# A transformer kernel of twenty stages on one core: norm and setup at the program's start reordered, and three weight splits of the sliding attention moved

## The chip, the cores and the metric

One core of a Trainium2 chip runs the whole program. The metric is the device time of one execution in microseconds (us); the kernel before has a median of 2272.48 us over three runs (2271.74 to 2279.61).

## What is computed

Four blocks one after the other over x of 512 tokens by 1024 features, float32: a sparse attention (nsa) and a differential attention, then an RWKV mixer with a feed-forward layer and a sliding-window attention with a second feed-forward layer. Cut to what the change touches: the first norm (with norm_pre[0]) and the sliding attention, in which `band` gives each block of 128 keys together with the one before:

```python
def rmsnorm(x, g):
    xf = x.astype(jnp.float32)
    y = xf * lax.rsqrt(jnp.mean(xf * xf, axis=-1, keepdims=True) + EPS)
    return (y * g.astype(jnp.float32)).astype(x.dtype)

def swa_sink_attention(x, k, v, w_q, sinks, w_o):
    q = (x @ w_q).reshape(B, nb, BLOCK, KV_HEADS, GROUP, HEAD_DIM)
    kb, vb = band(k), band(v)
    s = jnp.einsum('bnqhgd,bnkhd->bnhgqk', q, kb).astype(jnp.float32) * (HEAD_DIM ** -0.5)
    s = jnp.where(mask[None, :, None, None], s, NEG_INF)
    m = jnp.maximum(jnp.max(s, axis=-1, keepdims=True), sk)
    p = jnp.exp(s - m)
    denom = jnp.sum(p, axis=-1, keepdims=True) + jnp.exp(sk - m)
    o = jnp.einsum('bnhgqk,bnkhd->bnqhgd', (p / denom).astype(vb.dtype), vb)
    return o.reshape(B, T, ATTN_HEADS * HEAD_DIM) @ w_o
```

Beside that, a table of 32 relative-distance biases is spread over distances with a one-hot matrix for the first two attentions.

## The kernel before

**Split products.** Every float32 operand of a projection is held as two fp32r parts: a high part (rounded by ScalarE) and a low part (the rest, by GpSimd for weights and by VectorE for activations). A projection multiplies high with high, low with high and high with low (`project_features`, L334 to L361: 24 matmuls of 128x512 for each weight load of 128 columns; `project_tokens` for outputs by token). Weights come in loads of 512 KB into a ring of three raw slots (`fetch`, L255, on the SP queue, which waits for the low split of the load that had the slot). ScalarE's `split_hi` (L266, the instruction at L278) and GpSimd's `split_lo` (L282, at L289) fill a ring of three pairs of parts. A part's slot is reused when the projection three loads back is done. Where the calls to `split_hi` and `split_lo` stand in each engine's program decides when each load is split.

**Stages.** The program is a list of stages, each with a method for TensorE (`tensor`), ScalarE (`scalar`), VectorE (`vector`) and GpSimd (`gpsimd`). Behind each stage every engine signals; unless a flag such as `scalar_goes_on` is set, it then waits for the other three (`end_stage`, L3186).

**The start.** `Setup` (L503) loads x (2 MB, one load), constants, the bias table and the one-hot matrix, and sixteen small pieces of vectors into rows (L528 to L549), splits the table in three bf16 parts on VectorE, and turns the rows with six transposes (L559) and copies (L595). Then, behind a barrier, `Norm` (L694) runs: GpSimd issues the load of the gain (L629); for each of the four tiles of 128 tokens ScalarE squares (L634), takes the root (L636) and scales (L654), VectorE multiplies with the gain (L644) and inverts (L649), TensorE turns the tile with eight transposes (L663), ScalarE makes the high part (L673) and VectorE the low part (L681). Behind another barrier the first projection begins (`NsaProject`, L931). After its first twelve weight loads TensorE makes the biases: eight groups of 32 small matmuls (L571) in banks 4 to 7, each copied out by VectorE (L602).

**The sliding attention.** `SwaProject` (L2046) makes the queries: eight weight loads, with the first two pairs' scores ahead of the last one. `SwaAttend` (L2098) then goes over 32 pairs u (eight pairs of heads by four blocks of 128 queries, the block without a predecessor last). For each: two score matmuls per pair of heads (L2134, TensorE), masked minimum on VectorE (L2256), exponential on ScalarE (L2143), reciprocal of the sum on VectorE (L1310), scaling on GpSimd (L2234; `sink` at L2227 puts the sink column in), transposes on TensorE (`turn`, L2156, three pairs behind the scores), a copy by VectorE (L2265) or ScalarE (L2199), values on TensorE (L2168, one more pair behind). Every fourth pair the result is split in high (L2203) and low (L2269). At the steps 11, 19 and 27 ScalarE and GpSimd each split one of the first three loads of the output's weights:

```python
    SPLITS = [11, 19, 27]
...
            if u in self.SPLITS:
                self.env.split_lo(pool, self.ahead - 2 + self.SPLITS.index(u))
            if u < n_pairs:
                sink(u)
            if u >= 2:
                scale(u - 2)
```

The next stage, `Output` (L727), multiplies with those weights, slice by slice (L386 high parts, L396 low part), beginning when the last low part of the attention's result is there.

Of the kernel before, what the change touches and what calls it, by code (L numbers as in the profile page):

```python
# [14 lines left out]
P = 128  # L15
T = 512
# [486 lines left out]
class Setup(Stage):  # L503


    def __init__(self, env):
        super().__init__(env)
        self.bias = env.take(HEADS, T, at=env.words - HEADS * T)
        at = env.area
        self.rows = env.take(6, P, at=at)  # L510
        self.tab = env.take(HEADS, at=at + 1000)
        self.tab_rest = env.take(HEADS, at=at + 1016)
# [3 lines left out]
        self.x_arrived = env.sem("x_arrived")  # L516
# [35 lines left out]
    def tensor(self, pe):  # L552
        env, nc = self.env, self.env.nc
        pe.wait_ge(self.rows_arrived, 16 * self.N_ROWS)
        pe.wait_ge(self.const_arrived, 16)
        pe.wait_ge(self.tab_arrived, 64)
        for n in range(6):
            size = [128, 56, 88, 88, 88, 88][n]
            tr = nc.tensor.transpose(env.ps[:, n // 4, (n % 4) * P:(n % 4) * P + size], self.rows[0:size, n, :],  # L559
                                     env.ident[0:size, 0:size])  # L560
# [14 lines left out]
    def vector(self, dve, step):  # L575
        env, nc = self.env, self.env.nc
        nc.vector.memset(env.eps, EPS)
        nc.vector.memset(self.tab[:], 0.0).then_inc(self.rows_zeroed, 1)
        dve.wait_ge(self.tab_arrived, 64)
        dve.wait_ge(self.rows_zeroed, 1)  # L580

# [8 lines left out]
        nc.vector.memset(self.table3[96:128, :], NEG).then_inc(self.table_ready, 1)  # L590
        dve.wait_ge(self.vec_ready, 1)
        o = 0
        for n in range(6):
            size = [128, 56, 88, 88, 88, 88][n]
            step(nc.vector.tensor_copy(env.vec[:, o:o + size], env.ps[:, n // 4, (n % 4) * P:(n % 4) * P + size]))  # L595
            o += size

# [13 lines left out]
class Renorm:  # L611
# [27 lines left out]
    def gain(self, dve, i):  # L639

        env, nc = self.env, self.env.nc
        if self.g_row is not None:
            dve.wait_ge(env.next_g_arrived, 16 * self.g_n)
            nc.vector.tensor_tensor(self.un[:, i, :], env.x[:, i, :], env.next_g, ALU.mult)  # L644

# [48 lines left out]
class Norm(Stage):  # L694


    def __init__(self, env, g_row, u, x_arrived):
        super().__init__(env)
        self.norm, self.x_arrived = Renorm(env, g_row, u), x_arrived
# [5 lines left out]
    def scalar(self, act, step):  # L705
        act.wait_ge(self.x_arrived, 16)
        for i in range(NT):
            self.norm.square(act, step, i)
            self.norm.unit(act, i)
        self.env.split_hi(act, 1)  # L710
        for i in range(NT):
            self.norm.high(act, i)

    def vector(self, dve, step):
        for i in range(NT):
            self.norm.gain(dve, i)
            self.norm.invert(dve, i)
        for i in range(NT):
            self.norm.low(dve, i)

    def tensor(self, pe):
        for i in range(NT):
# [208 lines left out]
class NsaProject(Stage):  # L931
# [19 lines left out]
    def tensor(self, pe):  # L951
        env, nc = self.env, self.env.nc
        u = self.m.u
        for ld, g in self.q + self.kvc:
            project_features(env, pe, ld, u, g)
        self.setup.bias_tensor(pe)

        pe.wait_ge(self.setup.bias_taken, 8)
# [7 lines left out]
    def vector(self, dve, step):  # L966
        self.setup.bias_vector(dve, step)
# [900 lines left out]
class FfnUp(Stage):  # L1868
# [4 lines left out]
    def __init__(self, env, layer, m):  # L1873
# [9 lines left out]
        n = str(layer)  # L1883
        self.scaled, self.scaled_before = m.scaled, 2 * FT * layer
        self.gelu_done, self.gelus_before = m.gelu_done, FT * layer
        self.product_ready = env.sem("product_ready" + n)
        self.act_hi_ready, self.act_done = env.sem("act_hi_ready" + n), env.sem("act_done" + n)
# [5 lines left out]
    def wait_result(self, pe, k):  # L1893
        pe.wait_ge(self.act_done, k + 1)
# [13 lines left out]
    def scalar(self, act, step):  # L1908
        env, nc, m = self.env, self.env.nc, self.m

        def gelu(j):
            act.wait_ge(env.proj_taken, self.g0 + 2 * j + 2)
            if j >= 2:
                act.wait_ge(self.act_done, j - 1)
            nc.scalar.activation(m.gelu[:, j % 2, :], m.conv[:, 2 * (j % 2), :], ACT.Gelu_apprx_tanh).then_inc(self.gelu_done, 1)

        def act_hi(j):
            act.wait_ge(self.product_ready, j + 1)
# [1400 lines left out]
```

## Time and profile before

| | |
|---|---|
| median of three runs | 2272.48 us |
| profiled execution: its time / its span | 2274.92 us / 2273.0 us |
| TensorE busy | 2070.1 us, 91% |
| ScalarE / VectorE / GpSimd busy | 41% / 37% / 40% |
| mean granted TensorE clock | 0.937 of 2.4 GHz |
| share of the last chain on TensorE | 79% |

TensorE's busy time is the length of the program but for a tenth. An engine's idle time matters only where TensorE waits for it. In the rows, PE is TensorE, ACT ScalarE, DVE VectorE, POOL GpSimd, SP the queue of the loads.

### The profile page before, as it was taken

To read this page: it belongs to the slowest core of one execution; us is meant where nothing else is said; L and a number is where in the kernel's file an instruction comes from. 1 tells how busy PE (TensorE), PEld (TensorE's weight loads), DVE (VectorE), ACT (ScalarE), POOL (GpSimd) and SP (SyncE) were. 2 spreads that over 40 slices of the span, in tenths; PEclk is the share of its full clock that TensorE was granted. 3 is DMA by queue.
4 is the path that set the end of the run, shared out by engine and by line. 5 is a ranking of instruction groups with operands and counts; after the bars stand their busy time and mean duration, and the time that the engine had idled before them with its cause. 6 is when DMAs were issued, how large, how long until landed. Compare 5 with 4: busy or idle time off the path is not lost.

```text
span 2273.0 us, 33586 instructions
## 1 busy us (share of the span) xinstructions
PE 2070.1 (91%) x13582; PEld 1661.5 (73%) x13582; DVE 848.5 (37%) x1813; ACT 935.9 (41%) x1707; POOL 915.2 (40%) x636
## 2 busy tenths in 40 slices
PE   4999999999997968997588899999999899999998
PEld 3889756788765746776477588888878568888886
DVE  2100467340027375146565353333033524334301
ACT  3431477453247354443133353444143535344422
POOL 2431267534446322341012734455434542544542
PEclk9987999999998969898589999999999999999999
DMA  4322100123310211221210323333322121333332
GB/s 119 93 78 65 47 20 2 48 69 101 93 56 19 70 42 49 76 75 38 49 31 19 101 62 98 102 93 111 102 75 84 38 66 56 102 97 98 103 111 74
DMA packets 222361, 161.05 MB, mean 71 GB/s; under 512 B 30631, under 2 KB 205295, under 8 KB 222208
## 3 DMA queue, kind: packets, MB, share of 16 engines
q1 hardware_dynamic: 220016, 151.83, 22.6%
q0 software_dynamic: 2192, 7.07, 1.0%
q8 instruction: 109, 1.79, 0.3%
q14 instruction: 44, 0.36, 0.1%
HBM read 153.64 MB, written 5.24 MB: 70 GB/s over the span
## 4 chain that ended last, share of the span: by engine, by line
PE 79%; DVE 9%; ACT 4%; POOL 3%; issue 3%; DMA 1%; POOLq 1%; SPq 0%; DVEq 0%; PEld 0%; PEldq 0%; ACTq 0%
PE ps L386 15%; PE ps L348 13%; PE ps L350 13%; PE ps L359 13%; PE ps L396 7%; PE ps L1355 2%; PE ps L1368 2%; PE ps L1344 2%; POOL weights_lo L289 1%; DVE ps L901 1%; DVE buffer L906 1%; PE ps L1082 1%; PE ps L2892 1%; PE ps L2156 1%; PE ps L1703 1%
## 5 line engine op out<-in xcount | busy, mean ns | idle before, releaser
L289 POOL TENSOR_TENSOR weights_lo<-buffer,weights_hi 128x1024 fp32r<-128x1024 f32 (+1 forms) x265 | 654.0, 2470 | 981.4 <-ACT weights_hi L278 981.2
L278 ACT ACTIVATE weights_hi<-buffer 128x1024 fp32r<-128x1024 f32 (+1 forms) x265 | 276.4, 1045 | 340.7 <-PE ps L396 285.5
L348 PE MATMUL ps<-u_hi,weights_hi 128*128 128x512 f32 (+1 forms) x752 | 278.5, 378 | 5.6 <-DVE u_lo L681 3.0
L350 PE MATMUL ps<-u_lo,weights_hi 128*128 128x512 f32 (+1 forms) x736 | 274.8, 377 | 0.0
L1931 ACT ACTIVATE buffer<-ps,buffer 128x512 f32<-128x512 f32 x88 | 68.7, 781 | 276.4 <-PE ps L359 276.4
L359 PE MATMUL ps<-u_hi,weights_lo 128*128 128x512 f32 (+1 forms) x752 | 177.2, 378 | 0.0
L1961 DVE SCALAR_TENSOR_TENSOR buffer<-ps,buffer,buffer 128x511 f32<-128x511 f32 x88 | 66.0, 750 | 287.7 <-ACT buffer L1931 287.7
L348 PEld LDWEIGHTS ps<-u_hi,weights_hi 128*128 128x128 f32 x752 | 141.2, 190 | 32.0 <-issue 5.6
L350 PEld LDWEIGHTS ps<-u_lo,weights_hi 128*128 128x128 f32 x736 | 138.4, 188 | 25.5
L359 PEld LDWEIGHTS ps<-u_hi,weights_lo 128*128 128x128 f32 x752 | 137.0, 191 | 25.8
L2932 ACT ACTIVATE buffer<-ps 32x256 f32<-32x256 f32 (+5 forms) x96 | 47.7, 498 | 152.9 <-PE ps L2892 68.1
L386 PE MATMUL ps<-weights_hi,act_hi 128*128 128x512 f32 x352 | 108.8, 390 | 0.5 <-issue 0.5
L386 PE MATMUL ps<-weights_hi,act_lo 128*128 128x512 f32 x352 | 108.4, 389 | 0.0
L1430 POOL TENSOR_SCALAR buffer<-buffer,buffer,buffer 128x512 f32<-128x512 f32 (+3 forms) x128 | 76.4, 609 | 41.2 <-DVE buffer L1310 41.2
L396 PE MATMUL ps<-weights_lo,act_hi 128*128 128x512 f32 x352 | 92.8, 389 | 0.0
L900 DVE RECIPROCAL buffer<-buffer 128x1 f32<-128x1 f32 x24 | 3.9, 162 | 230.8 <-ACT buffer L827 230.7
L348 PE MATMUL ps<-nsa_u_hi,weights_hi 128*128 128x512 f32 x192 | 82.7, 431 | 7.5 <-PEq L3188 5.7
L1389 ACT ACTIVATE buffer<-buffer,buffer 128x512 f32<-128x512 f32 (+3 forms) x128 | 71.4, 558 | 30.1 <-DVE buffer L1463 29.2
L350 PE MATMUL ps<-nsa_u_lo,weights_hi 128*128 128x512 f32 x192 | 80.6, 420 | 0.0
L348 PE MATMUL ps<-diff_u_hi,weights_hi 128*128 128x512 f32 (+1 forms) x216 | 77.6, 373 | 3.3 <-ACT weights_hi L278 2.2
L386 PEld LDWEIGHTS ps<-weights_hi,act_hi 128*128 128x128 f32 x352 | 65.7, 188 | 15.5 <-issue 2.1
L1463 DVE CUSTOM_DVE_ANT_0 buffer<-ps,buffer 128x512 f32<-128x512 f32 (+3 forms) x128 | 61.9, 486 | 38.3 <-PE ps L1344 36.0
(403 smaller groups left out, 4277.5 us busy)
## 6 DMA issues: line engine op xcount, KB each, us to landing
buffer<-in_w_up SPq DMA_DIRECT2D x88, 512.0 KB, 3.8
buffer<-in_w_down SPq DMA_DIRECT2D x44, 512.0 KB, 3.4
buffer<-in_diff_w_in SPq DMA_DIRECT2D x32, 512.0 KB, 4.0
buffer<-in_nsa_w_in SPq DMA_DIRECT2D x28, 512.0 KB, 3.8
buffer<-in_w_rkv SPq DMA_DIRECT2D x24, 512.0 KB, 4.1
buffer<-in_nsa_w_out SPq DMA_DIRECT2D x8, 512.0 KB, 3.5
buffer<-in_diff_w_out SPq DMA_DIRECT2D x8, 512.0 KB, 3.6
buffer<-in_w_o_rwkv SPq DMA_DIRECT2D x8, 512.0 KB, 3.4
```

Source lines behind the costliest of these rows:

```text
L278: self.nc.scalar.activation(self.part_hi[:, part % self.PARTS, 0:n], self.raw[:, ld % self.RAW, 0:n], ACT.Copy).then_inc(self.hi_ready, 1)
L289: self.nc.gpsimd.tensor_tensor(self.part_lo[:, part % self.PARTS, 0:n], self.raw[:, ld % self.RAW, 0:n], self.part_hi[:, part % self.PARTS ...
L348: nc.tensor.matmul(out, hi[:, k, :], rhs[0][:, k, tokens], start=(k == 0), stop=False)
L350: nc.tensor.matmul(out, hi[:, k, :], rhs[1][:, k, tokens], start=False, stop=False)
L359: mm = nc.tensor.matmul(out, lo[:, k, :], rhs[0][:, k, tokens], start=False, stop=(k == KD - 1))
L386: nc.tensor.matmul(out(i, b), lhs[part][:, index * m + k, i * P:(i + 1) * P], hi[:, k, b * width:(b + 1) * width], start=(index + k == 0 a ...
L396: mm = nc.tensor.matmul(out(i, b), lhs[0][:, index * m + k, i * P:(i + 1) * P], lo[:, k, b * width:(b + 1) * width], start=False, stop=stop)
L1389: nc.scalar.activation(m.p[:, at, 0:n], m.p[:, at, 0:n], ACT.Exp, scale=-1.0, bias=m.nmax[:, at:at + 1], accum_out=m.psum[:, at:at + 1]).t ...
L1430: nc.gpsimd.tensor_scalar(p, p, m.scale[:, at:at + 1], m.gate[:, i, gate:gate + 1], ALU.mult, ALU.mult).then_inc(self.p_scaled, 1)
L1463: nc.vector.tensor_tensor_reduce(m.p[:, at, 0:n], self.banks(u)[:, st, 0:n], m.bias[:, 2 * k + st, T - n:T], -1.0, 1e38, ALU.add, ALU.min, ...
L1931: nc.scalar.activation(m.conv[:, 2 * (j % 2) + half, :], env.bank(g), ACT.Identity, scale=self.col(2, half, j), bias=self.col(3, half, j)) ...
L1961: step(nc.vector.scalar_tensor_tensor(c[:, 1:T], env.bank(g)[:, 0:T - 1], self.col(1, half, j), c[:, 1:T], ALU.mult, ALU.add))
```

## The change

At the start: x comes in three loads, the first three weights are fetched ahead of the small loads (`load_vectors`), the first two stages have no barrier, and ScalarE loads the root's table at once. VectorE scales a tile with gain and reciprocal in one instruction (`scale`), in place of ScalarE's `unit` and VectorE's `gain`. The table's preparation, the rows' transposes (now in banks 6 and 7) and their copies move into `NsaProject`, ahead of the biases. The scratch of `Setup` moves to another place in memory.

In the sliding attention: the split at step 11 moves into the query projection behind the last query weight's split (j = 6), those at 19 and 27 behind the last pair. In `FfnUp` both layers share five semaphores, which count on (`tiles_before`); no instruction moves there.

```diff
@@ Setup
-        self.x_arrived = env.sem("x_arrived")
+        self.tensor_goes_on = self.scalar_goes_on = self.vector_goes_on = self.gpsimd_goes_on = True
+        self.x_arrived = [env.sem(f"x_arrived{i}") for i in range(3)]
...
     def load(self, sp):
         env, io, nc = self.env, self.env.io, self.env.nc
-        sp.dma_start(env.x, io["x"].rearrange("b (t p) d -> p (b t) d", p=P)).then_inc(self.x_arrived, 16)
-        sp.dma_start(env.const, io["shape_constants"]).then_inc(self.const_arrived, 16)
+        for i, end in enumerate((1, 2, NT)):
+            sp.dma_start(env.x[:, i:end, :],
+                         io["x"][0, i * P:end * P, :].rearrange("(t p) d -> p t d", p=P)).then_inc(self.x_arrived[i], 16)
+            if i == 0:
+                sp.dma_start(env.const, io["shape_constants"]).then_inc(self.const_arrived, 16)
+
+    def load_vectors(self, sp):
+        io = self.env.io
         sp.wait_ge(self.rows_zeroed, 1)
...
     def bias_tensor(self, pe):
 
         env, nc = self.env, self.env.nc
+        pe.wait_ge(self.tab_arrived, 64)
+        pe.wait_ge(self.table_ready, 1)
         for i in range(8):
-            if i >= 4:
-                pe.wait_ge(self.bias_taken, i - 3)
+            if i >= 2:
+                pe.wait_ge(self.bias_taken, max(i - 2, 1))
...
+    def scale(self, dve, i):
+
+        env, nc = self.env, self.env.nc
+        dve.wait_ge(env.next_g_arrived, 16 * self.g_n)
+        dve.wait_ge(env.rstd_ready, self.n + i + 1)
+        nc.vector.scalar_tensor_tensor(self.un[:, i, :], env.x[:, i, :], self.rstd[:, i:i + 1], env.next_g,
+                                       ALU.mult, ALU.mult).then_inc(env.un_ready, 1)
@@ Norm
+        self.tensor_goes_on = self.scalar_goes_on = self.vector_goes_on = self.gpsimd_goes_on = True
...
     def scalar(self, act, step):
-        act.wait_ge(self.x_arrived, 16)
-        for i in range(NT):
-            self.norm.square(act, step, i)
-            self.norm.unit(act, i)
-        self.env.split_hi(act, 1)
-        for i in range(NT):
-            self.norm.high(act, i)
+        env, norm = self.env, self.norm
+        act.wait_ge(self.setup.rows_zeroed, 1)
+        env.nc.scalar.activation(env.sqrt_junk, env.eps, ACT.Sqrt)
+
+        def square(i):
+            act.wait_ge(self.setup.x_arrived[min(i, 2)], 16)
+            norm.square(act, step, i)
+
+        for i in range(3):
+            square(i)
+        norm.high(act, 0)
+        square(3)
+        norm.high(act, 1)
+        env.split_hi(act, 0)
+        norm.high(act, 2)
+        norm.high(act, 3)
+        env.split_hi(act, 1)
 
     def vector(self, dve, step):
         for i in range(NT):
-            self.norm.gain(dve, i)
             self.norm.invert(dve, i)
-        for i in range(NT):
-            self.norm.low(dve, i)
+            self.norm.scale(dve, i)
+            if i:
+                self.norm.low(dve, i - 1)
+        self.norm.low(dve, NT - 1)
@@ NsaProject
         for ld, g in self.q + self.kvc:
             project_features(env, pe, ld, u, g)
+        self.setup.vectors_tensor(pe)
         self.setup.bias_tensor(pe)
...
     def vector(self, dve, step):
+        self.setup.table_vector(dve, step)
+        self.setup.vectors_vector(dve, step)
         self.setup.bias_vector(dve, step)
@@ SwaProject
-        self.env.split_lo(pool, self.q[-1][0])
+        self.env.split_lo(pool, self.q[-1][0] + 1)
...
-            env.split_hi(act, min(ld + 1, self.q[-1][0]))
+            env.split_hi(act, min(ld + 1, self.q[-1][0]) + (j >= KD - 2))
@@ SwaAttend
-    SPLITS = [11, 19, 27]
...
-            if u in self.SPLITS:
-                env.split_hi(act, self.ahead - 2 + self.SPLITS.index(u))
...
         high(KD - 1)
+        env.split_hi(act, self.ahead)
...
-            if u in self.SPLITS:
-                self.env.split_lo(pool, self.ahead - 2 + self.SPLITS.index(u))
...
+        self.env.split_lo(pool, self.ahead)
@@ build, SP queue
             for ld in range(len(env.loads)):
                 env.fetch(sp, ld)
+                if ld == env.RAW - 1:
+                    setup.load_vectors(sp)
```

VectorE at the start of the program, the kernel before (`buffer_51` is the scaled tile, `buffer_49` x, `buffer_60` the gain, `buffer_56` the turned vectors):

```order
L595 COPY buffer_56<-ps 128x88 x4
L644 TENSOR_TENSOR buffer_51<-buffer_49,buffer_60 128x1024
L649 RECIPROCAL buffer_58<-buffer_58 128x1
...
L681 TENSOR_TENSOR nsa_u_lo<-ps,nsa_u_hi 128x8x128 x4
L602 COPY buffer_61<-ps 128x32x16 x8
```

and of the change, from the second tile's reciprocal to the bias copies:

```order
L671 RECIPROCAL buffer_58<-buffer_58 128x1
L665 SCALAR_TENSOR_TENSOR buffer_51<-buffer_49,buffer_58,buffer_60 128x1024
L703 TENSOR_TENSOR nsa_u_lo<-ps,nsa_u_hi 128x8x128
L671 RECIPROCAL buffer_58<-buffer_58 128x1
L665 SCALAR_TENSOR_TENSOR buffer_51<-buffer_49,buffer_58,buffer_60 128x1024
L703 TENSOR_TENSOR nsa_u_lo<-ps,nsa_u_hi 128x8x128
L671 RECIPROCAL buffer_58<-buffer_58 128x1
L665 SCALAR_TENSOR_TENSOR buffer_51<-buffer_49,buffer_58,buffer_60 128x1024
L703 TENSOR_TENSOR nsa_u_lo<-ps,nsa_u_hi 128x8x128 x2
...
L608 COPY buffer_56<-ps 128x88 x4
L616 COPY buffer_61<-ps 128x32x16 x8
```

The low parts of tiles 0 and 1 now stand between the scalings of tiles 1, 2 and 3, and the copies of the vectors have left the place ahead of them for one ahead of the bias copies.

GpSimd in the sliding attention, the kernel before, from the last split of the query projection to pair 0 and around step 11:

```order
L289 TENSOR_TENSOR weights_lo<-buffer_52,weights_hi 128x1024 x8
L2227 COPY buffer_162<-buffer_165 128x2 x3
L2234 TENSOR_SCALAR buffer_162<-buffer_162,buffer_168,buffer_55 128x256 x2
...
L289 TENSOR_TENSOR weights_lo<-buffer_52,weights_hi 128x1024
L2227 COPY buffer_162<-buffer_165 128x2
```

and of the change, at the beginning and at the end of the attention:

```order
L289 TENSOR_TENSOR weights_lo<-buffer_52,weights_hi 128x1024 x9
L2260 COPY buffer_162<-buffer_165 128x2 x3
L2267 TENSOR_SCALAR buffer_162<-buffer_162,buffer_168,buffer_55 128x256 x2
...
L2267 TENSOR_SCALAR buffer_162<-buffer_162,buffer_168,buffer_55 128x128 x2
L289 TENSOR_TENSOR weights_lo<-buffer_52,weights_hi 128x1024 x2
L896 DMA buffer_57<-in_norm_g 128x1024
```

A ninth split stands in the query projection, none among the pairs, and two ahead of the load of the output's gain.

## Rows read from the trace of the kernel before

**Rows 1.** Chain of waits, 0 to 120 us: start us, length us, what

```profile
13.40 1.55 PE ps L559 x6
17.00 4.10 DMA buffer<-in_norm_pre
39.64 0.77 PE ps L348
40.40 0.43 PE ps L350
```

**Rows 2.** Timeline, 0 to 75 us: start, length, engine, line, operation

```profile
14.98 1.67 DVE L595 COPY buffer<-ps 128x128 f32<-128x128 f32 x6 [2.94 <-PE ps L559]
22.41 1.21 DVE L644 TENSOR_TENSOR buffer<-buffer,buffer 128x1024 f32<-128x1024 f32 x1
23.58 1.04 ACT L634 ACTIVATE buffer<-buffer 128x1024 f32<-128x1024 f32 x1
24.75 0.29 ACT L636 ACTIVATE buffer<-buffer 128x1 f32<-128x1 f32 x1
29.22 1.97 PE L663 MATMUL ps<-buffer,buffer 128*128 128x128 f32 x8 [0.78 <-ACT buffer L654]
33.72 3.74 ACT L673 ACTIVATE nsa_u_hi<-ps 128x1024 fp32r<-128x1024 f32 x4
34.75 4.62 DVE L681 TENSOR_TENSOR nsa_u_lo<-ps,nsa_u_hi 128x1024 fp32r<-128x1024 f32 x4 [4.02 <-ACT nsa_u_hi L673]
```

**Rows 3.** DMA view, 0 to 20 us: rate in 40 slices; one load

```profile
GB/s 0 0 0 90 57 123 344 426 393 360 426 434 418 418 401 410 398 369 371 233 134 125 64 112 308 310 315 347 306 290 291 290 290 209 33 0 49 147 385 352
...
buffer<-in_x SPq DMA_DIRECT2D x1, 2048.0 KB, 8.0
```

**Rows 4.** Timeline, 105.5 to 117.5 us

```profile
106.47 6.71 PE L571 MATMUL ps<-table,one_hot 128*128 128x16 bf16 x256
...
107.53 7.38 DVE L602 COPY buffer<-ps 128x512 f32<-128x512 f32 x8 [68.17 <-PE ps L571]
```

**Rows 5.** Chain of waits, 1765 to 1850 us

```profile
1765.07 0.23 PE ps L348
...
1780.59 0.37 PE ps L2156 x2
...
1783.55 0.59 PE ps L2156 x4
...
1787.17 0.38 PE ps L2156 x2
...
1793.69 1.14 PE ps L2156 x4
...
1811.60 1.13 PE ps L2156 x4
...
1831.09 1.13 PE ps L2156 x4
...
1844.66 5.54 PE ps L386 x16
```

**Rows 6.** Waits of TensorE, 1774 to 1846 us: total us, times, longest

```profile
PE ps L2156 <- POOL buffer L2234: 10.4, 4, 3.6
```

**Rows 7.** Timeline of GpSimd, 1725 to 1875 us

```profile
1763.56 2.39 POOL L289 TENSOR_TENSOR weights_lo<-buffer,weights_hi 128x1024 fp32r<-128x1024 f32 x1 [3.05 <-ACT weights_hi L278]
...
1808.44 2.35 POOL L289 TENSOR_TENSOR weights_lo<-buffer,weights_hi 128x1024 fp32r<-128x1024 f32 x1 [2.54 <-ACT weights_hi L278]
```

**Rows 8.** Windows: PE, PEld, DVE, ACT, POOL busy, granted clock, DMA

```profile
1774.00:1787.00 13.00, 12.59 (x107) 7.79 (x106) 9.86 (x45) 9.97 (x34) 8.18 (x21) 1.00 0.01 1
...
1812.00:1823.00 11.00, 11.00 (x77) 6.76 (x76) 6.24 (x26) 6.71 (x22) 6.21 (x17) 0.74 0.12 44
```

**Rows 9.** Costliest groups of the page

```profile
L278 ACT ACTIVATE weights_hi<-buffer 128x1024 fp32r<-128x1024 f32 (+1 forms) x265 | 276.4, 1045 | 340.7 <-PE ps L396 285.5
```

**Rows 10.** Timeline of ScalarE, 1758 to 1776 us

```profile
1767.99 1.28 ACT L2143 ACT_TABLE_LOAD   x1
```

More of the change, by code:

```diff
@@ L550, with vectors_tensor @@
     N_ROWS = 3 + 4 + 3 + 6
-    def tensor(self, pe):
+    def vectors_tensor(self, pe):
         env, nc = self.env, self.env.nc
         pe.wait_ge(self.rows_arrived, 16 * self.N_ROWS)
-        pe.wait_ge(self.const_arrived, 16)
-        pe.wait_ge(self.tab_arrived, 64)
         for n in range(6):
             size = [128, 56, 88, 88, 88, 88][n]
-            tr = nc.tensor.transpose(env.ps[:, n // 4, (n % 4) * P:(n % 4) * P + size], self.rows[0:size, n, :],
+            tr = nc.tensor.transpose(env.ps[:, 6 + n // 4, (n % 4) * P:(n % 4) * P + size], self.rows[0:size, n, :],
                                      env.ident[0:size, 0:size])
@@ L575, in vector, with table_vector @@
     def vector(self, dve, step):
-        env, nc = self.env, self.env.nc
-        nc.vector.memset(env.eps, EPS)
+        nc = self.env.nc
+        nc.vector.memset(self.env.eps, EPS)
         nc.vector.memset(self.tab[:], 0.0).then_inc(self.rows_zeroed, 1)
+    def table_vector(self, dve, step):
+        nc = self.env.nc
         dve.wait_ge(self.tab_arrived, 64)
@@ L590, in vector, with vectors_vector @@
         nc.vector.memset(self.table3[96:128, :], NEG).then_inc(self.table_ready, 1)
+    def vectors_vector(self, dve, step):
+        env, nc = self.env, self.env.nc
         dve.wait_ge(self.vec_ready, 1)
@@ L594, in vector @@
             size = [128, 56, 88, 88, 88, 88][n]
-            step(nc.vector.tensor_copy(env.vec[:, o:o + size], env.ps[:, n // 4, (n % 4) * P:(n % 4) * P + size]))
+            cp = nc.vector.tensor_copy(env.vec[:, o:o + size], env.ps[:, 6 + n // 4, (n % 4) * P:(n % 4) * P + size])
             o += size
+        cp.then_inc(self.bias_taken, 1)
     def bias_vector(self, dve, step):
@@ L694, with __init__ @@
 class Norm(Stage):
-    def __init__(self, env, g_row, u, x_arrived):
+    def __init__(self, env, g_row, u, setup):
         super().__init__(env)
-        self.norm, self.x_arrived = Renorm(env, g_row, u), x_arrived
+        self.norm, self.setup = Renorm(env, g_row, u), setup
+        self.tensor_goes_on = self.scalar_goes_on = self.vector_goes_on = self.gpsimd_goes_on = True
     def gpsimd(self, pool, step):
@@ L1893, in wait_result @@
     def wait_result(self, pe, k):
[L1894 removed]
+        pe.wait_ge(self.act_done, self.tiles_before + k + 1)
     def tensor(self, pe):
@@ L1959, in vector @@
                 c = m.conv[:, 2 * (j % 2) + half, :]
-                dve.wait_ge(self.scaled, self.scaled_before + 2 * j + half + 1)
+                dve.wait_ge(self.scaled, 2 * (self.tiles_before + j) + half + 1)
                 step(nc.vector.scalar_tensor_tensor(c[:, 1:T], env.bank(g)[:, 0:T - 1], self.col(1, half, j), c[:, 1:T],
@@ L1983, in __init__ @@
         self.conv, self.gelu = take(4, 512), take(2, 512)
-        self.scaled, self.gelu_done = env.sem("up_scaled"), env.sem("gelu_done")
+        self.signals = [env.sem(name) for name in ("up_scaled", "gelu_done", "product_ready", "act_hi_ready", "act_done")]
 class SwaMemory:
@@ L3205, in build @@
             setup,
-            Norm(env, pre[0], m.u, setup.x_arrived),
+            Norm(env, pre[0], m.u, setup),
         ]
```

27 lines of the change are left out of this document (13 added, 14 removed).

## Prediction

> **What bounds the kernel now.** The page comes first: TensorE is busy for most of the span, so time can only be won where it is idle or slow. Two such places matter here. The chain of waits of the opening shows that the first projection matmul starts at 39.64 us [rows 1]. Ahead of it lie two pieces in a row: the wait for sixteen small loads with six transposes behind them (13.40 us), and a fresh start by GpSimd's load of the norm's gain, issued at 17.00 behind the stage barrier and 4.10 us long. Behind that barrier ScalarE squares, scales and splits x tile by tile [rows 2]. The second place is the sliding attention. Its chain [rows 5] should be read by L2156, the four transposes ("turn") of one of 32 pairs. From pair 3's at 1780.59 to pair 7's at 1787.17 four pairs take 6.58 us, with TensorE alone on the chain. But the turns of pairs 9, 17 and 25 come late, each behind a low split on GpSimd (L289). The waits view puts 10.4 us of TensorE's idle time on GpSimd's scaling in this stage [rows 6], and GpSimd's timeline shows why: a 2.35 us split sits just ahead of it [rows 7].
>
> **The opening.** x becomes three loads (tile 0, tile 1, tiles 2 and 3), the barriers of the first two stages go, the gain's load is issued at once, and the small loads move behind the first three weights. The 2 MB of x land 8.0 us after their issue, and the data row shows about 400 GB/s once it flows [rows 3]. Tile 0 is a quarter: 3.9 us less (1.5 MB at 400), so it lands near 4.9, or 5.5 if the gain's 0.5 MB interleave with it. Tiles 2 and 3 now have the constants (0.32 MB) and the gain (0.5 MB) ahead of or beside them: 8.8 + 2.0 = 10.8 at worst; I take 10.7. The square with its root takes 1.46 us (23.58 to the end of the root at 25.04) [rows 2]. ScalarE's own scaling (L654) is gone: one VectorE instruction now does gain and scale. It isn't in the trace; its nearest rows are the gain multiply of the same size, 1.21 us [rows 2], from below, and nothing excludes that it costs a tenth more. I take 1.25.
> Step by step, in the written order: ScalarE squares tile 2 from 10.7 to 12.2, and splits tile 0 (3.74/4 = 0.94) to 13.1; VectorE takes tile 0's low part (4.62/4 = 1.16) to 14.3. Only then come, on VectorE's queue, the reciprocal and scale of tile 2 (to 15.8), low part 1 (17.0), and the scale of tile 3 (18.4). TensorE turns tile 3 in 1.97 us, to 20.4; ScalarE's high part ends at 21.4, VectorE's low part at 22.5. All durations are of rows 2. TensorE starts at **22.5 instead of 39.64: 17.1 us**. Ends: if the gain doesn't hinder x (8.8), 20.6, so 19.0 us; if the loads are 2 us later than taken, 15.1 us. The second root table load (one of two) is gone too, but it lay under the wait.
> What is moved goes to the end of the first twelve projections. There six transposes and six copies now stand between the last projection and the bias copies. Before, the table's matmuls began at 106.47 and VectorE's eight copies ran from 107.53 to 114.91 [rows 4]. Now the transposes come first (at most their 1.55 us at the start of the program [rows 1]; about half of it behind a running projection, 0.8), then the six copies, 1.67 us [rows 2], and only then the eight, for which the first two groups of matmuls are ready. So the copies start 0.8 + 1.67 + 0.1 = 2.6 us after the projections in place of 1.06: **1.5 us lost**; with waits for the copied banks I take 1.9 (ends 1.0 and 3.2). The small loads' twenty issues on SP now stand ahead of the fourth weight's fetch, which must wait for the first low split anyway, near 19 us. Before, all of them had landed by 13.40 [rows 1]; shifted by two pieces of x and three weights they are issued well before 19, so they cost nothing, and three projections of TensorE would cover a fetch that is some us late. The table's preparation on VectorE moves behind the norm, where it is idle until the bias. The shared semaphores of the two feed-forward layers change no wait.
> On splitting x, the Trainium skill speaks against the change: "DMA: Bandwidth & Descriptors", section "Bandwidth", says to batch loads to 1 MiB or more for 75% of the peak and gives 341 GB/s at 1 MB. By that, as an estimate, x would take 6.2 us of transfer in place of 5.2 and this term would be about 1 us smaller; the trace has no x load in pieces.
>
> **The attention.** Its three splits of the output's weights go: one behind the last of the query projection's, two behind the last pair. What they cost: pair 5 turned at 1783.55, so pair 9 was due at 1790.13 and came at 1793.69: 3.56 us. From pair 9 to 17 17.91 us passed, and from 17 to 25 19.49, where eight pairs take 2 x 6.58 = 13.16: 4.75 and 6.33 us lost [rows 5]. These include slow stretches: the granted clock is 0.74 between 1812 and 1823, so partly at 1.2 GHz in place of 2.4, after TensorE had idled; it is 1.00 before the first stall [rows 8]. Behind pair 25 four transposes again take 1.13 us, as behind pair 9: some 1.5 us. Sum 16.1 us. Can the others keep TensorE's pace? In the 13 us before the first stall VectorE was busy 9.86, ScalarE 9.97, GpSimd 8.18 [rows 8]: each about three quarters, none of them the bound, but little slack for a chain over four engines. I take **15.0 us**; the lower end is GpSimd's own time, 3 x 2.35 = 7 us, the upper 16.1.
> The moved ones: in the query projection GpSimd's last split starts at 1763.56 and ends at 1766.0 [rows 7]. One more (2.4) ends at 1768.4, ScalarE's (1.05, row of the page [rows 9]) before it. Next in GpSimd's queue stand the sinks for the first exponentials. These can't start before ScalarE's table load ends at 1769.3 [rows 10]: hidden, with under 1 us to spare, and behind it lies a whole projection of TensorE. At the end two splits are done on ScalarE 2.1 us after its last high part, and on GpSimd 1.05 + 2 x 2.35 = 5.8 us after it. TensorE's first output slice there takes from 1844.66 on 5.54 us for its high parts [rows 5] and eight low ones of 0.23, 7.3 in all, longer than that, and needs only the slice split in the projection; the second is ready in time: **0**. If the cover were gone, up to 4.7 us.
>
> **The sum.** 17.1 - 1.9 + 15.0 - 0 = 30.2 us. Against the profiled execution's 2274.92 (span 2273.0) that is 2244.7. The median of the three runs is 2.4 us below that execution, so I forecast **2242.3 us**, 1.3% faster.
>
> **Rivals.**
> 1. The attention finds another bound: without the splits, the loop from scores over VectorE, ScalarE, VectorE, GpSimd and back is late for every pair, and only 7 us come back: 2250. For it: three engines three quarters busy. Against: from pair 3 to pair 7 the chain shows no wait of TensorE [rows 5]. Chance 0.13.
> 2. The opening yields half: the gain's load, made by GpSimd, shares the engines with x, const and 1.5 MB of weights and lands late, or the pieces of x do. The first scale then waits; with everything of 10 us landed at 15, TensorE starts near 27: 12.6 - 1.9 + 15 = 25.7 us, 2247. Against: the data row shows 400 GB/s from 3.5 us on [rows 3], so all that TensorE's start needs is in by then. Chance 0.08.
> 3. The change doesn't do what it says at the attention's end: the two splits wait for something (slot, load) and the Output waits for them: 4.7 us lost, 2247. Against: their slots are freed by the query projection's last splits, as before, and a whole attention lies between. Chance 0.04.
> 4. Slower. TensorE starts earlier but on thin work (eight transposes per tile), and stays at 1.2 GHz. A matmul then takes 0.43 us in place of 0.23 [rows 1, 5]; 30.2 us are used up after 151 such matmuls, little more than six projections of 24. If all twelve of the opening ran so, 288 x 0.2 = 58 us would be lost: 2300. Against: after 39.64 only the first handful took 0.43, behind just as thin transposes. Chance 0.02. The Trainium skill ("TensorE: Matmul & The Clock Gate", part on the clock gate) reports a clock seen stuck low for tens of us; no run here shows it.
>
> **How the numbers follow.** Forecast 0.73, rivals 0.13, 0.08, 0.04 and 0.02. The ends of the terms give 2236 (19.0 - 1.0 + 16.1, with 2 us of full clock behind the attention) to 2256 (15.1 - 3.2 + 7 - 2). I give 2234 to 2254: it holds the first three rivals and leaves out the slower one and any two mishaps together. 0.5% (11.4 us) is what a measurement can tell from no change; for a gain below that, both parts must fail by more than half: 0.03. Slower by over 0.5%: 0.02. Faster: 0.95.
>
> **What would show it.** First projection matmul at 21 to 24 us; VectorE's eight bias copies starting 2 to 3 us after the twelfth projection; no L289 on GpSimd among the pairs and turns four pairs apart every 6.6 us, granted clock 1.00 there; the attention from first turn to Output shorter by 15 us; Output's first two slices without a wait for weights. It is wrong if TensorE starts after 27 us, if turns four pairs apart take more than 7.5 us, or if the rest of the program changes length.

## The result, and the profile after

The changed kernel has a median of **2244.59 us** (2240.5 to 2245.11, 4 runs) against 2273.86 before in the same comparison: ratio 0.9859, 95% interval 0.9838 to 0.9879. The forecast was 2242.3 us, with a range of 2234 to 2254. The profiled execution has a span of 2242.8 us, 30.2 less than before.

The chain of waits of the changed kernel, 0 to 120 us, answers to [rows 1]:

```profile
2.13 9.57 DMA buffer<-in_x
11.73 1.16 ACT buffer L648 x2
13.20 0.92 ACT nsa_u_hi L695
14.15 1.22 DVE nsa_u_lo L703
15.55 1.28 DVE buffer L665
16.83 1.13 DVE nsa_u_lo L703
18.14 2.72 DVE buffer L665
20.90 1.98 PE ps L685 x8
22.91 1.03 ACT nsa_u_hi L695
23.96 1.24 DVE nsa_u_lo L703
25.29 0.79 PE ps L348
...
92.80 0.77 PE ps L565 x6
93.60 1.03 DVE buffer L608 x6
94.63 6.42 DVE buffer L616 x7
101.05 0.87 DVEq L3220
101.96 0.79 PE ps L348
```

TensorE starts its first projection at 25.29 in place of 39.64, and goes on behind the biases at 101.96. The same point of the kernel before was 114.97 in its chain. The last link of x (tiles 2 and 3) lands at 11.73, and from there the steps follow in the order of the prediction. One of them is over twice its length: VectorE's fourth scaling, 2.72 us. Its timeline (start, length, engine, line, operation; in brackets how long the engine had idled and for what), with GpSimd's beside it:

```profile
5.86 0.16 DVE L671 RECIPROCAL buffer<-buffer 128x1 f32<-128x1 f32 x1 [4.93 <-ACT buffer L650]
8.97 1.28 DVE L665 SCALAR_TENSOR_TENSOR buffer<-buffer,buffer,buffer 128x1024 f32<-128x1024 f32 x1 [2.95 <-DMA buffer<-in_norm_pre]
...
17.42 2.35 POOL L289 TENSOR_TENSOR weights_lo<-buffer,weights_hi 128x1024 fp32r<-128x1024 f32 x1 [15.35 <-ACT weights_hi L278]
...
18.14 2.71 DVE L665 SCALAR_TENSOR_TENSOR buffer<-buffer,buffer,buffer 128x1024 f32<-128x1024 f32 x1
```

The gain's load landed late as well: the first scaling waited 2.95 us for it. Whether that counts is for an experiment.

In the sliding attention the chain, 1735 to 1825 us, answers to [rows 5]; L2190 is now the turn, L2168 the scores, L2202 the values:

```profile
1760.28 1.81 PE ps L359 x8
...
1768.62 0.37 PE ps L2190 x2
...
1775.19 0.37 PE ps L2190 x2
...
1781.78 0.37 PE ps L2190 x2
...
1788.39 0.37 PE ps L2190 x2
...
1794.97 0.37 PE ps L2190 x2
...
1801.55 0.37 PE ps L2190 x2
...
1808.16 0.37 PE ps L2190 x2
...
1816.46 3.92 PE ps L386 x16
```

The first line is the end of the query projection (1762.09). The turns are those of the pairs 3, 7, 11 and so on to 27: one every 6.57 to 6.61 us, with TensorE alone on the chain between them. The Output's first high parts take 3.92 us where they took 5.54. The windows view of the attention says the same (columns as in [rows 8]): granted clock 1.00 throughout.

```profile
1762.00:1816.46 54.46, 52.20 (x457) 32.31 (x457) 44.36 (x181) 41.17 (x140) 36.10 (x90) 1.00 0.01 2
```

TensorE's waits, 1762 to 1840 us (us in total, times, longest), beside [rows 6]: 0.2 us on GpSimd where it was 10.4.

```profile
PE ps L386 <- DVE swa_u_lo L2301: 1.4, 1, 1.4
PE ps L2190 <- POOL buffer L2267: 0.2, 1, 0.2
```

The span's 30.2 us, by points of the two chains. Of the kernel before, these lines end the twelve projections (106.63), begin the projection behind the biases, and end the query projection (1774.06):

```profile
104.81 1.81 PE ps L359 x8
...
114.97 0.80 PE ps L348
...
1772.25 1.81 PE ps L359 x8
```

| stretch | before | after | gained |
|---|---|---|---|
| start to first projection | 39.64 | 25.29 | 14.35 |
| twelve projections | 66.99 | 67.51 | -0.52 |
| their end to the projection behind the biases | 8.34 | 9.16 | -0.82 |
| from there to the end of the query projection | 1659.09 | 1660.13 | -1.04 |
| to the Output's first matmul (attention) | 70.60 | 54.37 | 16.23 |
| the rest | 428.34 | 426.34 | 2.00 |

### The profile page after: what moved, and what is told of

It is laid out like the page before. It is cut to its first block, busy times and chain, and to the rows that moved or that the text cites. A ratio compares the mean times of both kernels' runs of the same rounds, so it can differ in the third digit from the quotient of the medians.

```text
span 2242.8 us, 33583 instructions
## 1 busy us (share of the span) xinstructions
PE 2062.9 (92%) x13582; PEld 1658.4 (74%) x13582; DVE 850.3 (38%) x1813; ACT 930.6 (41%) x1703; POOL 917.2 (41%) x636
## 4 chain that ended last, share of the span: by engine, by line
PE 80%; DVE 9%; ACT 3%; POOL 3%; issue 3%; DMA 1%; POOLq 1%; SPq 0%; DVEq 0%; PEld 0%; PEldq 0%; ACTq 0%
PE ps L386 15%; PE ps L348 13%; PE ps L350 13%; PE ps L359 13%; PE ps L396 8%; PE ps L1393 2%; PE ps L1406 2%; PE ps L1382 2%; DVE ps L936 1%; DVE buffer L941 1%; POOL weights_lo L289 1%; PE ps L1120 1%; PE ps L2168 1%; PE ps L2924 1%; PE ps L2190 1%
## 5 line engine op out<-in xcount | busy, mean ns | idle before, releaser
L289 POOL TENSOR_TENSOR weights_lo<-buffer,weights_hi 128x1024 fp32r<-128x1024 f32 (+1 forms) x265 | 654.6, 2472 | 974.7 <-ACT weights_hi L278 974.5
L1427 ACT ACTIVATE buffer<-buffer,buffer 128x512 f32<-128x512 f32 (+3 forms) x128 | 71.4, 558 | 30.2 <-DVE buffer L1501 29.3
```

Source lines behind the costliest of these rows:

```text
L289: self.nc.gpsimd.tensor_tensor(self.part_lo[:, part % self.PARTS, 0:n], self.raw[:, ld % self.RAW, 0:n], self.part_hi[:, part % self.PARTS ...
L1427: nc.scalar.activation(m.p[:, at, 0:n], m.p[:, at, 0:n], ACT.Exp, scale=-1.0, bias=m.nmax[:, at:at + 1], accum_out=m.psum[:, at:at + 1]).t ...
```

## The experiments

The first four kernels ask whether the change is two independent savings or whether one depends on the other, and what set the start of the first projection.

**open_only**: the change with the attention as before (its splits at the steps 11, 19 and 27 again).

```diff
-            env.split_hi(act, min(ld + 1, self.q[-1][0]) + (j >= KD - 2))
+            env.split_hi(act, min(ld + 1, self.q[-1][0]))
...
+            if u in self.SPLITS:
+                env.split_hi(act, self.ahead - 2 + self.SPLITS.index(u))
```

> The change's opening with the attention's splits as in the kernel before. Theory (two independent parts): the span is 13 us below the kernel before (first projection near 25.3 us, the rest of the program as before within 1 us), time near 2261, ratio 0.994; the attention from the end of the query projection to the Output again 70.6 us. Rival (the opening's shift alone changed what the attention meets, for instance where the clock falls): the attention comes out below 66 us, or the whole gain is not 13 but over 18.

Measured: median 2263.43, ratio 0.995 (0.9935 to 0.9964), profiled span 2256.6. First projection at 24.84, the one behind the biases at 101.94, the attention 70.61 us. The profiled execution is 5 us shorter than the other three (2263.3 to 2263.8), and its part from there to the end of the query projection took 1655.9 us where 1659.1 within 1 us was expected; that part comes back under lo_late_again.

**attend_only**: the kernel before with the attention's part of the change.

> The kernel before with the attention's splits moved as in the change. Theory: the attention shrinks from 70.6 to 54.4 us, the Output's first slice by 1.6, span 17 to 18 us below before, time near 2256, ratio 0.992; together with the other run the two savings add up to the change's 29 within 2 us. Rival (moved splits cost elsewhere when the opening is the old one): under 14 us.

Measured: median 2256.3, ratio 0.9925 (0.9908 to 0.9942), profiled span 2251.7; the attention 54.36 us, the Output's first high parts 3.93. The median lies 17.2 us below the kernel before in that comparison, as expected; the profiled span lies 21.3 below, more than the expected 17 to 18. The two ratios multiply to 0.9875, the change's is 0.9859 (0.9838 to 0.9879), so the savings add up within the intervals (10.1 and 17.2 us by the medians, 27.3 in sum, where 29 within 2 was expected). The attention is the same to 0.01 us with either opening: 70.60 and 70.61 with the splits inside, 54.37 and 54.36 without. The rival, that it depends on when it begins, is out.

**lo_late**: ScalarE's first weight split one place later, so that GpSimd's low split no longer runs beside the scaling of tile 3.

```diff
         norm.high(act, 1)
-        env.split_hi(act, 0)
         norm.high(act, 2)
+        env.split_hi(act, 0)
         norm.high(act, 3)
```

> The change, with ScalarE's first weight split (and with it GpSimd's low split) one place later, behind the high part of tile 2. Theory (in the change the scaling of tile 3 took 2.71 us in place of 1.28 because GpSimd's low split, from 17.42 to 19.77, ran on the same memory ports): the fourth scaling takes 1.28 and the first projection starts at 23.8 to 24.0 in place of 25.29; the low part of tile 3, which reads the accumulator banks, keeps its 1.22 though the split now runs beside it. Rival (the loads of weights slowed it): the fourth scaling stays over 2 us and the start near 25.3.

Measured: the timeline, 10 to 26 us:

```profile
17.55 1.28 DVE L665 SCALAR_TENSOR_TENSOR buffer<-buffer,buffer,buffer 128x1024 f32<-128x1024 f32 x1
...
20.36 2.34 POOL L289 TENSOR_TENSOR weights_lo<-buffer,weights_hi 128x1024 fp32r<-128x1024 f32 x1 [18.29 <-ACT weights_hi L278]
...
21.96 1.23 DVE L703 TENSOR_TENSOR nsa_u_lo<-ps,nsa_u_hi 128x1024 fp32r<-128x1024 f32 x1 [1.37 <-ACT nsa_u_hi L695]
...
23.29 0.79 PE L348 MATMUL ps<-nsa_u_hi,weights_hi 128*128 128x512 f32 x1 [2.42 <-DVE nsa_u_lo L703]
```

The scaling takes 1.28 us with GpSimd's split out of its way, though the loads of weights are where they were, so the rival is out. The low part, which has the split beside it from 21.96 to 22.70, keeps its 1.23. TensorE starts at 23.29: 1.43 of the 2.0 us from the scaling, the rest because the last of x landed at 11.14 here. So the theory holds as far as it was tried: VectorE's scaling, with x and the gain both read from SBUF, is held up by GpSimd's two-input subtraction; VectorE's low part, with one of its inputs in the accumulator banks, isn't. The single time, 2239.43, is 5 us below the change's median; lo_late_again takes that up.

**scale_first**: VectorE's low parts one tile later.

```diff
             self.norm.scale(dve, i)
-            if i:
-                self.norm.low(dve, i - 1)
+            if i >= 2:
+                self.norm.low(dve, i - 2)
+        self.norm.low(dve, NT - 2)
         self.norm.low(dve, NT - 1)
```

> The change, with VectorE's low parts one tile later, so that the scalings of tiles 2 and 3 no longer stand behind the low parts of tiles 0 and 1. Theory (the order on VectorE's queue, not the loads alone, sets the start): scaling of tile 2 at 13.5 in place of 15.55, of tile 3 by 16.2 and so ahead of GpSimd's split, first projection at 21.5 to 22.2. Rival (the landing of x at 11.73 sets it whatever the order): start after 24 us.

Measured: scaling of tile 2 at 12.98, of tile 3 at 15.58, each a little earlier than expected, and the latter ahead of GpSimd's split; first projection at 21.31, the one behind the biases at 97.83.

```profile
16.90 2.36 POOL L289 TENSOR_TENSOR weights_lo<-buffer,weights_hi 128x1024 fp32r<-128x1024 f32 x1 [14.83 <-ACT weights_hi L278]
...
21.31 0.79 PE L348 MATMUL ps<-nsa_u_hi,weights_hi 128*128 128x512 f32 x1 [2.42 <-DVE nsa_u_lo L703]
```

The start is 4.0 us ahead of the change's: 0.5 because the last of x landed at 11.21, 1.43 because the fourth scaling no longer meets the split, and the other 2.0 is the order itself. But the span is 2241.9, only 0.9 less than the change's: of the 4.1 us lead behind the biases, 3.2 are gone by the end of the query projection, in instructions that are the same.

The next four ask what each split costs, and what x in pieces brings.

**all_behind**: all three splits behind the last pair (the two lines of `SwaProject` undone).

> The change, with the first split too behind the last pair (none in the query projection). Theory (the splits behind the last pair are hidden by the Output's first slice): the attention 54.4 to 54.8 us, since only the high split of the first slice is now late by some 0.3 us; GpSimd's three low splits end 7 us behind the last high part, each before TensorE asks for it. Rival (what stands behind the last pair is exposed): 2 us or more are lost between the last high part and the Output's second slice.

Measured: the attention 54.67 us, 0.3 more; TensorE's wait ahead of the Output is 1.7 us on the high split in place of 1.4 on the last low part. GpSimd's timeline has its three low splits from 1815.75 on:

```profile
1815.75 7.12 POOL L289 TENSOR_TENSOR weights_lo<-buffer,weights_hi 128x1024 fp32r<-128x1024 f32 x3 [3.46 <-ACT weights_hi L278]
```

They end at 1822.87, and the part behind the Output's first matmul is 426.39 us, as in the change (426.34). What stands behind the last pair is hidden but for the 0.3 us, and these are what moving the first split into the query projection brings.

**one_back**: one split again at step 19.

```diff
+            if u == 19:
+                env.split_hi(act, self.ahead - 1)
...
+            if u == 19:
+                self.env.split_lo(pool, self.ahead - 1)
```

> The change, with one split (the output's second load) back at step 19 of the attention. Theory (each split among the pairs stalls TensorE by 3.6 us and a stretch at 1.2 GHz follows): the attention takes 54.4 + 3.6 + 1 to 3 = 59 to 61 us. Rival (only the third of three in a row hurts, or only where VectorE is late too): below 57 us.

Measured: the attention 60.46 us, 6.1 more. The waits view (1750 to 1835 us) has 3.1 us of it, and the slow clock behind it the rest, as the windows and the chain show:

```profile
PE ps L2190 <- POOL buffer L2269: 3.3, 2, 3.1
```

```profile
1796.00:1808.00 12.00, 8.89 (x56) 5.17 (x53) 5.53 (x23) 5.70 (x18) 7.24 (x15) 0.72 0.14 44
1808.00:1820.00 12.00, 12.00 (x106) 7.32 (x104) 10.35 (x42) 9.46 (x34) 9.03 (x23) 1.00 0.01 2
```

```profile
1799.89 1.13 PE ps L2190 x4
...
1806.49 0.37 PE ps L2190 x2
```

The six groups between these two lines (two turns, two of values, two of scores) take 6.60 us at 1.2 GHz, where the same six take 3.62 at 2.4 GHz. So one split of 2.34 us on GpSimd costs 3.1 us of idle TensorE and 3.0 us of slow TensorE. A single one suffices, which puts out the rival that only the third in a row hurts.

**hi_early**: all three splits among the pairs, but ScalarE's high parts at the steps 8, 16 and 24, GpSimd's low parts at 11, 19 and 27.

```diff
+            if u + 3 in self.SPLITS:
+                env.split_hi(act, self.ahead - 2 + self.SPLITS.index(u + 3))
...
```

> The change's opening and all three splits among the pairs, but ScalarE's high part three steps ahead of GpSimd's low part (steps 8, 16, 24 and 11, 19, 27). Theory (GpSimd's wait for ScalarE's high part, 2.2 to 2.5 us in its queue, is half of each stall, its own 2.35 us the other half, less the slack of 0.5 to 1 us that it has per pair): stalls of 1 to 1.8 us in place of 3.6, the attention at 57 to 61 us in place of 70.6. Rival (GpSimd's own instruction alone makes the stall): over 65 us.

Measured: the attention 59.96 us, and the Output's first high parts 5.52 us, as slow as in the kernel before. TensorE's waits, 1750 to 1835 us, and one of GpSimd's three splits:

```profile
PE ps L2191 <- POOL buffer L2269: 3.2, 4, 1.3
```

```profile
1779.71 2.36 POOL L289 TENSOR_TENSOR weights_lo<-buffer,weights_hi 128x1024 fp32r<-128x1024 f32 x1
```

Three stalls of at most 1.3 us in place of three of up to 3.6 [rows 6], and no wait ahead of L289 where it was 2.54 us [rows 7]. Moving ScalarE's high parts alone brings back 10.7 of the 16.2 us that the change won here. In the kernel before, ScalarE made the first of them at 1789.42, behind the exponentials of pair 10, and GpSimd stood in its queue for it until 1790.55. The other 5.6 us are the splits themselves, with the slow clock behind the third stall; the clock behind the stalls is in both figures, so they don't price the wait alone.

**x_whole**: x in one load.

```diff
+        sp.dma_start(env.x, io["x"].rearrange("b (t p) d -> p (b t) d", p=P)).then_inc(self.x_arrived[0], 16)
+        sp.dma_start(env.const, io["shape_constants"]).then_inc(self.const_arrived, 16)
...
```

> The change, with x in one load, the constants behind it. Theory (pieces help because ScalarE's squares of tiles 0 and 1 run while the rest lands): x lands at about 10.5 with the gain beside it; four squares, then the turns follow: first projection 1.5 to 3 us later than 25.29. Rival (loads in pieces move slower, so that x in one load lands near 8.8 and all follows from there): first projection at 25.3 or earlier.

Measured: x lands at 10.54, all four squares behind it; first projection at 27.95, 2.66 us later than in the change, behind the biases 104.47. The pieces are worth about that; the six executions with the change's opening start between 24.60 and 26.03.

The last four ask what is left in the opening, and why a start 4 us earlier shortened the span by 1.

**after_again**: the change once more.

> The change as it is, beside the next kernel on one chip. The attention and the rest behind it as in its first profile (54.4 us; 426 us within 1), first projection 24.8 to 25.4; time 2240 to 2246. Theory (what differs between executions is how long the clock stands at 1.2 GHz, which the work does not decide alone): the span follows the total of the slow stretches, about half a us for each us of them.

Measured: median 2244.55, ratio 0.988 (0.9864 to 0.9897); single executions from 2241.41 to 2250.0. First projection at 24.92, the attention 54.37, the rest 425.45.

**scale_first_lo_late**: both rearrangements.

> Both rearrangements of the opening at once: low parts one tile later on VectorE, first weight split behind the high part of tile 2. Theory (in the first only VectorE's order counts, since its fourth scaling then ends before GpSimd's split begins): first projection at 21.0 to 21.6, no earlier than with VectorE's order alone; the biases end 3.5 to 4.5 us earlier than in the change; median 2 to 5 us below the change's, about 2240. Rival (the gains add, 2 us from the split's place and 4 from VectorE's order): first projection near 19.5.

Measured: first projection at 20.75, behind the biases 97.04, 4.9 us ahead of the change's first profile and 4.2 ahead of after_again (101.24). The gains don't add: 0.56 us earlier than scale_first, where "no earlier" was expected, of which 0.14 are x's landing and 0.42 that tile 3's turns took 1.55 us in place of 1.97.

```profile
16.78 1.55 PE L685 MATMUL ps<-buffer,buffer 128*128 128x128 f32 x8 [1.49 <-DVE buffer L665]
```

Median 2243.55, ratio 0.9875 (0.9859 to 0.9892): 1.0 us below after_again in place of the expected 2 to 5, no difference that these runs can tell.

**gain_on_sp**: the gain's load on SP's queue between tiles 0 and 1 of x.

```diff
             if i == 0:
+                sp.dma_start(env.next_g, io["norm_pre"][0].partition_broadcast(P)).then_inc(self.gain_arrived, 16)
+            if i == 1:
                 sp.dma_start(env.const, io["shape_constants"]).then_inc(self.const_arrived, 16)
...
```

> The change, with the norm's gain loaded by SP's queue between tiles 0 and 1 of x, the constants behind tile 1. Theory (GpSimd issues its load at 1.36 us and it shares the engines, so that it lands at 8.97 and the first scaling waits 2.95 us; but tiles 2 and 3 of x set the start): the gain lands at 5.5 to 7, the first scaling starts near 7, tiles 2 and 3 land within 0.5 us of 11.7, and the first projection still starts at 24.5 to 25.5. Rival (the gain's landing sets the start): over 1.5 us earlier.

Measured: the first scaling starts at 6.35 in place of 8.97, the last of x lands at 11.30, and the first projection starts at 24.86.

```profile
6.35 1.28 DVE L668 SCALAR_TENSOR_TENSOR buffer<-buffer,buffer,buffer 128x1024 f32<-128x1024 f32 x1 [0.22 <-DMA buffer<-in_norm_pre]
```

The 2.95 us wait for the gain cost nothing: the last of x sets the start. (Tile 0's turn, ready earlier, waited for the constants until 8.73, which this edit moves back; that is off the path too.) The span of this execution, 2247.8, is 5 us above the change's: 6.0 us are lost between 102 us and the end of the query projection (1666.1 us there, 1660.1 in the change), where not one instruction differs, and 1.1 won behind it.

**lo_late_again**: lo_late, now timed.

> The kernel with the first weight split one place later once more, now timed. Theory (its low time of the first look, 2239.4, was half its 2 us earlier start and half a favourable share of slow clock): median 2241 to 2244, at most 2 us below the change's 2244.6, the bias end 2 to 2.5 us earlier than in the change. Rival (a real gain of 5 us): median at or below 2240.

Measured: median 2246.29, ratio 0.9878 (0.9862 to 0.9894), against 2272.99 before in that comparison: outside the expected 2241 to 2244, on the other side from the rival. The two profiled executions of this one kernel differ by 12.9 us. Their clock rows (span, mean granted clock), of lo_late and of lo_late_again:

```profile
core 0: 2237.5 us, clock 0.938
```

```profile
core 0: 2250.4 us, clock 0.932
```

The projection behind the biases starts at 99.44 and 99.83, the attention takes 54.36 in both, the rest 425.38 and 426.01; the query projection ends at 1757.76 and 1770.03. A mean clock of 0.938 and 0.932 stands for 277 and 306 us at half clock (twice the missing share of the span). So 29 us more at 1.2 GHz go with 13 us of span. Windows from the projection behind the biases to the end of the query projection (behind the length, TensorE's busy time):

```profile
99.44:1757.76 1658.32, 1516.03 (x10664) 1212.90 (x10664) 656.90 (x1427) 692.35 (x1298) 655.48 (x446) 0.92 0.22 65
```

```profile
99.83:1770.03 1670.20, 1527.99 (x10664) 1223.88 (x10664) 654.20 (x1427) 692.05 (x1298) 655.82 (x446) 0.92 0.22 64
```

The same 10664 matmuls keep TensorE busy for 12.0 us more, and the part is 11.9 us longer: the matmuls run slower, the waits don't grow. For this pair that is the theory's half us for each us at 1.2 GHz. A mean clock of a whole execution is too coarse to foretell its time, though: two executions of after_again with 0.936 had spans of 2242.3 and 2248.2 us. What sets these stretches wasn't found. Nor is it settled whether an earlier start lengthens them by itself: with VectorE's new order the part took 1663.3 and 1663.1 us, in the change 1660.1 and 1661.8, in this one kernel 1658.3 and 1670.2.

## Why the prediction was right

**The sum.** Forecast 30.2 us below the profiled execution's 2274.92; the new profiled span is 30.2 less than the old. That is luck. Against the terms, the opening brought 2.75 us less, the biases 1.08 and the attention 1.23 more, 0.44 less in all; the places that had no term of their own brought 0.44 more (-0.52, -1.04 and 2.00). And four executions of after_again, the same kernel, have spans from 2239.4 to 2248.2. The range is the ends of the terms (2236 to 2256) moved down by 2 without a reason; the result lies in both.

**The opening: 17.1 forecast, 14.35 measured.** The mechanism and the order of the steps held, the size didn't: 14.35 lies below the term's own lower end, 15.1, and 25.29 misses the sign "21 to 24 us" (the prediction calls itself wrong only from 27 us on). "I take 10.7", "10.8 at worst" for tiles 2 and 3 of x: they landed at 11.73 (11.0 to 12.4 in the other kernels with x in pieces). The sum had the constants and the gain beside x, 2.95 MB in all, but not the three weights fetched right behind it. The windows view gives 288 GB/s as the mean up to the landing, 3.4 MB, some 0.4 MB more than that, which can hardly be anything but weights (the small loads were issued from 11.58 on). No run moved the weights, so their part in the delay isn't shown.

```profile
0.00:11.73 11.73, 1.33 (x7) 1.36 (x8) 2.51 (x6) 4.38 (x9) 0.91 (x5) 1.00 0.82 288
```

"I take 1.25" for each scaling: three took 1.28, the fourth 2.71, beside GpSimd's split; lo_late shows that this is the cause. These two are 2.5 of the 2.8 us. The prediction placed the fourth scaling and the first low split at the same time and didn't ask whether they disturb each other. That the gain might land late (rival 2) did come about, 8.97 us, but gain_on_sp shows it off the path. The small loads' issues were to be over well before 19 us; they ran from 11.58 to 21.09 and the fourth weight's fetch was issued at 21.13. The three projections in front covered that.

**What is moved to the biases: 1.9 forecast, 0.82 measured.** The six copies take 1.03 us in their new place, where the row of before gave 1.67, and the transposes 0.77. The copies for the biases start 1.75 us behind the last projection, 0.85 more than before (the sign said 2 to 3 us). Nothing waited for banks 6 and 7, so the 0.4 added for that was one margin too many.

**The attention: 15.0 forecast, 16.23 measured**, just above the upper end of 16.1. No other bound turned up (rival 1): VectorE 81%, ScalarE 76% and GpSimd 66% busy (44.36, 41.17 and 36.10 of 54.46 us) kept TensorE's pace. The prediction's "each about three quarters" was too high for GpSimd, whose 8.18 of 13 us are 63%. Near the end of the attention VectorE was busy 10.07 of 11 us without TensorE waiting:

```profile
1800.00:1811.00 11.00, 11.00 (x100) 6.85 (x97) 10.07 (x40) 8.75 (x32) 7.92 (x20) 1.00 0.01 2
```

**The moved splits: 0 forecast.** At the end that is right, and all_behind shows a reserve: three splits fit there for 0.3 us. The reason given for the one in the query projection was wrong in part. The sinks were to be there before ScalarE's table load ends, but ScalarE waits for them ahead of that load:

```profile
1756.84 1.28 ACT L2177 ACT_TABLE_LOAD   x1 [0.84 <-POOL buffer L2260]
```

The first exponential starts 2.8 us behind the seventh query projection in place of 2.0. The eighth projection (until 1762.09) hides it.

**The rest.** The 2 us that were kept for the range ("full clock behind the attention") came, 1.6 of them in the Output's first slice. Against them stand 1.04 us in the long middle and 0.52 in the twelve projections, places with the same instructions as before. In the projections the slow stretch lasted nine matmuls where before it was six; for the middle, lo_late's two executions show how far it goes by itself. The prediction called itself wrong if the rest of the program changed length; these changes are no more than one kernel shows between two executions, except the Output's slice, which it had named.

**The Trainium skill's rule** on batching loads to 1 MiB ("DMA: Bandwidth & Descriptors", section "Bandwidth") would not have tiles 0 and 1 of x as loads of 512 KB; its table is for loads issued by GpSimd, and x is issued by SP. x in one piece landed at 10.54, 1.2 us before the last of the change's three (0.5 to 1.9 over all kernels with pieces), so as to the landing the rule agrees with the trace, and with the prediction's estimate of 1 us; TensorE's start was still 2.66 us later, because nothing could be squared until all was there. Rival 4 (a clock that stays low) didn't come: after nine matmuls of the first projection they take 0.23 us again.

## What to carry to other kernels

A piece of foreign work in the queue of an engine that a pipeline over four engines passes through costs more than its own time: first the wait for its own input, which stands in the queue too, then the slow clock that follows TensorE's idle time (here 6 us for a 2.35 us instruction). Put it where a long run of one engine covers it, or at least let its input be ready three steps earlier. And when the same kernel varies by several us because of the clock, judge a small edit by the interval between two named instructions in the trace, and don't promise that interval in the span: 4.2 us there were 1.0 us of median here.

## What the runs showed that was not expected

- GpSimd's subtraction of two SBUF tiles (2.35 us) and VectorE's scaling of one (1.28 us) don't run side by side: the scaling that began 0.7 us into the split took 2.71 us and ended about 1.1 us after it. A VectorE cast of 128x16 that takes 0.17 us elsewhere took 1.96 beside the next split, and ended with it. VectorE's subtraction with one input in the accumulator banks kept its 1.22 us beside a split. The Trainium skill's "GPSIMD Engine Reference" (section "Specifications") lists the SBUF interfaces as shared with VectorE, with contention when VectorE runs in a two-port mode or reads two SBUF inputs; the scaling agrees with the second, and the cast, with one input only, could fall under the first, which no run here tried.

```profile
24.95 2.37 POOL L289 TENSOR_TENSOR weights_lo<-buffer,weights_hi 128x1024 fp32r<-128x1024 f32 x1 [5.19 <-ACT weights_hi L278]
...
25.39 1.96 DVE L592 CAST table_parts<-buffer 128x16 bf16<-128x16 f32 x1 [0.20 <-issue]
```

- The attention repeats to 0.03 us over nine executions of seven kernels with no split inside and the first one moved ahead (54.35 to 54.38), while the middle of the program, unchanged, differs by up to 12 us between two executions of one kernel.
